# Mixer of a decoder trunk: pooling products regrouped, the neighbour's cut to 16 columns, and 30 unread products ahead of the first rows

## What is computed

```python
POOL_WINDOWS = (2, 4, 8, 16)          # one window for each group of 256 columns
def _pool_mixer(x, hist, w, scale):
    ...
    for g, win in enumerate(POOL_WINDOWS):
        xg = xs[..., g * POOL_GROUP:(g + 1) * POOL_GROUP].astype(jnp.float32)
        ...
        outs.append((c[:, j + 1] - c[:, lo]) / cnt[None, :, None] - xg[:, p_len:])
    d = jnp.stack(outs, axis=2).astype(x.dtype)
    y = jnp.einsum('blgc,gce->blge', d, w).reshape(x.shape)
    return y * scale
```

## Time and profile before

| | us |
|---|---|
| median of 3 runs | 2530.28 (2530.12 to 2531.79) |
| the profiled execution | 2531.07 |
| its span in the trace | 2529.3 |
| TensorE busy in the span | 2396.9 (95%) |
| VectorE, ScalarE, GpSimd busy | 1292.2, 768.9, 342.9 |

### The profile page before, as it was taken

How to read it: one execution, slowest core, us unless ns; L and a number is a source line. 1 busy time by engine, 2 the same in 40 slices (tenths; PEclk the granted TensorE clock), 3 DMA queues, 4 the chain that set the end, 5 groups by cost and what they waited for, 6 DMA issues and landing times.

```text
span 2529.3 us, 35338 instructions
## 1 busy us (share of the span) xinstructions
PE 2396.9 (95%) x14022; PEld 2183.7 (86%) x14022; DVE 1292.2 (51%) x2398; ACT 768.9 (30%) x1477; POOL 342.9 (14%) x345
## 2 busy tenths in 40 slices
PE   7899999999999888999989888899999999999997
PEld 7899999999999788889987667588998989899996
DVE  4733443333344685776768778635244343333336
ACT  2331111111111234555546555412311111111112
POOL 1400000000000341000006545033000000000006
PEclk9899999999999999999999999799999999999998
DMA  5121110111111031000005444411211111111111
GB/s 163 42 62 39 50 45 24 47 50 50 50 50 63 13 115 42 19 19 5 8 22 176 149 155 157 155 47 34 67 51 34 51 51 32 36 51 51 51 42 68
DMA packets 137083, 154.00 MB, mean 61 GB/s; under 512 B 10256, under 2 KB 114224, under 8 KB 136808
## 3 DMA queue, kind: packets, MB, share of 16 engines
q1 hardware_dynamic: 124656, 110.07, 13.9%
q0 software_dynamic: 12288, 41.95, 5.2%
HBM read 142.24 MB, written 10.32 MB: 60 GB/s over the span
## 4 chain that ended last, share of the span: by engine, by line
PE 84%; DVE 10%; ACT 3%; issue 2%; DMA 1%; POOL 0%; SPq 0%; ACTq 0%; DVEq 0%
PE ps L216 24%; PE ps L218 23%; PE ps L217 23%; DVE split L209 5%; PE ps L2161 2%; PE ps L2126 2%; ACT split L204 2%; PE ps L2141 1%; PE ps L224 1%; PE ps L223 1%; PE ps L2142 1%; PE ps L1671 1%; PE ps L2148 1%; PE ps L580 1%; DVE plain L1914 1%
## 5 line engine op out<-in xcount | busy, mean ns | idle before, releaser
L216 PE MATMUL ps<-split 128*128 128x512 f32 (+6 forms) x3632 | 1236.9, 341 | 45.3 <-DVE split L209 17.6
L217 PE MATMUL ps<-split 128*128 128x512 f32 (+6 forms) x3632 | 1223.4, 337 | 0.0
L218 PE MATMUL ps<-split 128*128 128x512 f32 (+6 forms) x3632 | 1223.0, 337 | 0.0
L216 PEld LDWEIGHTS ps<-split 128*128 128x128 f32 x3632 | 690.0, 190 | 89.7 <-DVE split L209 21.2
L217 PEld LDWEIGHTS ps<-split 128*128 128x128 f32 x3632 | 690.4, 190 | 39.1 <-issue 2.5
L218 PEld LDWEIGHTS ps<-split 128*128 128x128 f32 x3632 | 690.8, 190 | 37.3
L204 ACT ACTIVATE split<-plain 128x1024 fp32r<-128x1024 f32 (+9 forms) x454 | 314.6, 729 | 594.1 <-PE ps L224 365.6
L209 DVE TENSOR_TENSOR split<-plain,split 128x344 fp32r<-128x344 f32 (+7 forms) x430 | 372.4, 890 | 182.7 <-ACT split L204 179.7
L1000 DVE TENSOR_TENSOR plain<-plain,ps 128x350 f32<-128x350 f32 (+1 forms) x132 | 68.0, 515 | 557.7 <-ACT plain L954 557.1
L276 DVE TENSOR_TENSOR plain<-plain,ps 128x512 f32<-128x512 f32 x360 | 244.7, 685 | 194.2 <-PE ps L218 189.4
L209 DVE TENSOR_TENSOR split<-ps,split 128x512 fp32r<-128x512 f32 (+5 forms) x480 | 247.1, 554 | 137.2 <-ACT split L204 135.1
(11 more groups left out here) (147 smaller groups left out, 1450.3 us busy)
## 6 DMA issues: line engine op xcount, KB each, us to landing
plain<-w_gate SPq DMA_DIRECT2D x44, 512.0 KB, 4.7
plain<-w_up SPq DMA_DIRECT2D x44, 512.0 KB, 4.0
plain<-w_down SPq DMA_DIRECT2D x44, 512.0 KB, 4.3
plain<-x_prompt SPq DMA_DIRECT2D x8, 512.0 KB, 11.3
x_spill<-plain SPq DMA_DIRECT2D x1, 4096.0 KB, 14.5
plain<-wo SPq DMA_DIRECT2D x8, 512.0 KB, 4.7
plain<-x_spill SPq DMA_DIRECT2D x8, 512.0 KB, 8.5
y_prompt<-plain SPq DMA_DIRECT2D x8, 512.0 KB
```

The source lines that it names most:

```text
L216: pe.matmul(out, still[0], moving[0], start=start, stop=False)
L217: pe.matmul(out, still[0], moving[1], start=False, stop=False)
L218: return pe.matmul(out, still[1], moving[0], start=False, stop=stop)
```

## The change

Three things change, all in TensorE's part of the mixer, and one instruction is added on VectorE.

- `pool_half` no longer alternates own and neighbour: it issues the four own products of a half, then the four of the neighbour. Only the first product of a half has `start=True`, and only the last `stop=True`, so a bank holds one accumulation.
- The neighbour's product has 16 columns (`reach = WINDOWS[-1]`) where it had 128. Samples and meta rows keep 24.
- Ahead of its first wait for data, TensorE issues 30 products of 512 fp32r columns into bank 5, which nobody reads; VectorE fills their operand with 1.0 by one memset.

```diff
+def keep_busy(pe, k, times, bank, rows, width):
+    for _ in range(times):
+        pe.matmul(k.ps[:, bank, 0:width], rows[:, 0:P], rows[:, 0:width], start=True, stop=True)
 def mixer_pe(pe, k):
     s, nt = k.s, k.ns + k.nm
+    pe.wait_ge(s["warm"], 1)
+    keep_busy(pe, k, 30, UNIT_BANKS[1], k.xt_hi[:, 0, :], BANK)
     pe.wait_ge(s["kept_in"], 16)
...
-        for j in range(4):
-            kc = 4 * half + j
-            g, cols = kc // 2, slice(kc * P, (kc + 1) * P)
-            if t < k.tiles:
-                out = k.ps[:, POOLED_BANKS[half], j * P:(j + 1) * P]
-                pe.matmul(out, k.x_main[:, t, cols], k.pool_band("here", g), start=True, stop=False)
-                if t:
-                    mm = pe.matmul(out, k.x_main[:, t - 1, cols], k.pool_band("before", g), start=False, stop=True)
...
+        n = P if t < k.tiles else nt
+        reach = WINDOWS[-1] if t < k.tiles else nt
+        for own in (True, False):
+            for j in range(4):
+                kc = 4 * half + j
+                g, cols = kc // 2, slice(kc * P, (kc + 1) * P)
+                out = k.ps[:, POOLED_BANKS[half], j * n:(j + 1) * n]
+                if own and t < k.tiles:
+                    pe.matmul(out, k.x_main[:, t, cols], k.pool_band("here", g), start=j == 0, stop=False)
+                elif own:
+                    pe.matmul(out, k.hist[:, cols], k.pool_band("hist", g), start=j == 0, stop=False)
+                elif t == k.tiles:
+                    mm = pe.matmul(out, k.x_tail[0:nt, cols], k.pool_band("meta", g)[0:nt], start=False, stop=j == 3)
+                elif t:
+                    mm = pe.matmul(out[:, 0:reach], k.x_main[:, t - 1, cols], k.pool_band("before", g)[:, 0:reach],
+                                   start=False, stop=j == 3)
...
         @block.vector
         def _(dve):
+            dve.memset(k.xt_hi[:, 0, 0:BANK].bitcast(F32), 1.0).then_inc(k.s["warm"], 1)
             page_index_dve(dve, k)
```

More of the change, by code:

```diff
@@ L574, in pool_half @@
             pe.wait_ge(s["pooled_lo"], n - 1)
-        for j in range(4):
-            kc = 4 * half + j
-            g, cols = kc // 2, slice(kc * P, (kc + 1) * P)
-            if t < k.tiles:
-                out = k.ps[:, POOLED_BANKS[half], j * P:(j + 1) * P]
-                pe.matmul(out, k.x_main[:, t, cols], k.pool_band("here", g), start=True, stop=False)
-                if t:
-                    mm = pe.matmul(out, k.x_main[:, t - 1, cols], k.pool_band("before", g), start=False, stop=True)
-                else:
[L584 to L588, removed]
+        n = P if t < k.tiles else nt
[14 more added lines that the diff above has]
+                                   start=False, stop=j == 3)
+                else:
+                    mm = pe.matmul(out[:, 0:reach], k.x_tail[0:nt, cols], k.pool_band("meta_before", g)[0:nt, 0:reach],
+                                   start=False, stop=j == 3)
         mm.then_inc(s["pooled"], 1)
```

## The result

The changed kernel takes 2514.03 us, the median of 4 runs (2513.20 to 2518.18); the kernel before took 2530.62 beside it (4 runs, 2530.12 to 2531.79). The ratio is 0.9938, with a 95% interval of 0.9922 to 0.9953. So it is 16.6 us faster, and 8.6 were forecast. The profiled execution took 2513.20, its span 2511.4, where before had 2531.07 and 2529.3: 17.9 us in the two profiles that the rest of this text compares.

What follows compares the result with a forecast made beforehand. Tile 0's serial chain was taken to bound the mixer's start, then VectorE and ScalarE at 7.06 us a step, VectorE's queue its end. Sum 7.7 - 0.4 + 0.1 + 1.2 = 8.6 us: 2522, range 2518.5 to 2526.5.

Steps and rivals of the forecast that it cites:

- Part 1: Program start: the 30 unread products run beside the transfers, from about 1.3 us; cost 0 to 0.6 us, taken 0.
- Part 2: Mixer, tile 0: grouped products at full clock, neighbours 0.21 us each; fold at 15.9 instead of 23.67, gain 7.7 us.
- Part 3: Mixer from unit 0: the clock of the 30 products is gone again; cost 0.4 us, range -2 to +1.5.
- rival D: Mixer start: clock kept up to unit 0, units and half-tile 2 us faster, 2520 us; chance 7%.
- Part 4: Mixer, tiles 1 to 7: 0.1 us per step off TensorE, covered by VectorE's 7.06; gain taken 0.1 us.
- Part 5: Mixer, last tile's halves: 3.4 us instead of 6.9, so VectorE's wait of 1.24 goes; gain 1.2 us.
- Rival E: After tile 0: head start given back by an unseen wait, late data or VectorE's queue; 2526 to 2530 us; chance 6%.
- Rivals B: Program start: the 30 products, all slow, end at 14.1 and delay tile 0; 2526.5 to 2529 us; chance 6%.
- C: Tile 0 on time but slow, clock lost before 10.7 or rising later; 2523 to 2525.7 us; chance 9%.
- A: Mixer steps: narrow products cost the clock, some 5.3 us a step, 2554 us in the end; chance 4%.

Runs made afterwards that it cites:

- the wide kernel: The changed kernel with neighbour products of 128 columns instead of 16, still regrouped: 2514.33 us, ratio to before 0.9939.
- The run that kept the clock: The changed kernel with 23 more unread 512-column products, 5 behind tile 0's halves and 18 ahead of unit 0: 2513.84 us, ratio to before 0.9941.
- 8 and 12 tiny products: The kernel before with 8 or 12 unread products of 8 by 8 at the start, one run each: 2541.90 us with 8, 2544.62 us with 12.
- regrouping alone: The changed kernel without the 30 unread products, their wait and the memset; pooling products stay regrouped and narrowed: 2523.50 us, ratio to before 0.9982.
- the thirty tiny products: The kernel before with 30 unread products of 8 by 8 at the start: 2522.72 us, ratio 0.9978.
- the counter-test: The changed kernel with 98 further unread products of 8 by 8 behind the 30, 256 instructions together: 2524.21 us, ratio to before 0.9979.

## Why the prediction was wrong

**What bounds the kernel: right for the mixer.** The serial chain of tile 0 was the place to look; VectorE's step of 7.06 and its queue at the end set the rest.

**Part 1, the 30 products as work: right.** They start at 1.47 (forecast 1.3) and the first rows' products at 10.91 (before 10.70), so they cost 0.2 of the 0 to 0.6 allowed; in the second profile of the changed kernel these start at 11.26, which is all of the 0.6.

**Part 2, tile 0: right in its mechanism, 0.5 too good.** Half 0 was ready at 13.1, not 12.7: it began 0.1 later than assumed, four own products took 1.06 us and four neighbours 0.99, where 0.9 and 0.85 were taken. The neighbour with 24 rows costs 0.25, inside the 0.1 to 0.33; the one with 128 rows costs 0.82 / 4 = 0.205. The fold came 7.21 earlier, with 7.7 forecast. The Trainium skill ("TensorE: Matmul & The Clock Gate", Back-to-back issue gap) gives a product of up to 64 columns some 60 cycles. From that the prediction worked out near 0.1 us for a neighbour, an estimate; the rows at 30.24 and 31.06 show twice that, and the wide kernel the same for eight times the columns.

**Part 3, clock lost by unit 0: right.** The windows read 0.50 from 17.00 to 26.90. Unit 0 is 7.20 earlier and the second unit 7.08 (34.93 to 27.85), so the loss was 0.1 instead of 0.4. The run that kept the clock shows rival D's price: 2.55 us at the first addition, not kept.

**Part 4, narrowed and regrouped products of tiles 1 to 7: 0.1 forecast, nothing measured** (the 0.1 to 0.2 us that narrowing gives come from tile 0). **Part 5, the wait of 1.24 at the last tile: gone,** as forecast. The mixer ends 8.50 ahead of before; the sum said 8.6. The lead is 7.2 at 60 us, where the terms gave 7.4, and the end adds 1.3 where 1.2 were forecast. That the sum fits so well is partly luck: part 2 gave 0.5 less than forecast, and part 3 cost 0.3 less.

**The step that failed** is the last: "FFN products that began at 109.50 now near 101, and the same 8.6 at the end." The first half of it held, the second did not: the lead went from 8.3 at 1920 us to 18.0 at 2333. Part 1 counted the 30 products as time on TensorE and asked only what they stand in front of. They are also 60 instructions in the program, and this effect was none of the parts, of the rivals or of the range. Rival E asked whether a head start could be given back; that it could grow was left out. The trace of before had the rows: six waits for "issue" in FFN 1, 7.2 us together, and 102 packets on the instruction queue, of which 27 lie at three branches of a loop. To have said that they would vanish was not possible from the trace alone (8 and 12 tiny products make them longer), but it showed 7.2 us of stalls whose cause was not an engine or a transfer of the kernel's data. That belongs into the range on both sides for any edit that adds or takes instructions.

Rivals B and C did not happen, since tile 0 began at 10.91 and its first half took 2.05 us against 3.79 without the warm-up. Nor did A: a window of after over four of the steps with narrow products shows the granted clock at 1.00.

```profile
40.00:70.00 30.00, 30.00 (x262) 29.83 (x261) 23.86 (x59) 15.06 (x25) 19.76 (x9) 1.00 0.01 2
```

One caution on sizes. The runs of before spread from 2522.9 to 2538.3 (28 runs on one chip), so medians of single edits carry an error of 1 to 2 us; regrouping alone has 6.1 by its median and 9.8 in its profiled run. The split of the 17.9 us into 8.3 ahead of FFN 1 and 9.7 in it comes from two profiles. The second profile of the changed kernel has 8.2 at 135 us, 9.5 at the first landmark and the same 9.7 in FFN 1: the part in FFN 1 is firm, the lead ahead of it moves by a us or two from profile to profile. That the second part hangs on position rests on the thirty tiny products, whose interval against before excludes no effect, and on the counter-test, whose interval (0.9965 to 0.9993) lies wholly above that of the changed kernel (0.9922 to 0.9953).

## What to carry to other kernels

Read the waits for "issue" and the packets of the instruction queue, stage by stage, before costing an edit: where a long loop is fetched anew at each return, any edit that changes the number of instructions ahead of it, on that engine, may remove those stalls or bring them on. To know what an edit is worth by its own merit, measure it beside a version with equally many instructions that do nothing. Where a chain starts the program, put products with the same shape of weights next to each other and keep TensorE working ahead of them. By the end of the mixer the two gave 6.4 and 2.6 us alone and 9.0 together.

## What the runs showed of the hardware

- Whether a loop body of 1624 TensorE instructions was fetched anew at its returns depended on where it begins: at all three returns in before, 9 packets of 16,384 bytes and 2.6 to 3.9 us each time, at none in after, and at two places at some of them. 60 instructions of no work ahead of it were worth 7 us of 2530.
- Such a gap can be booked under another engine: with 12 tiny products it reads as 14.4 us of waiting for VectorE.
- A pooling product with new 128-row weights took 0.205 us with 16 columns and 0.20 with 128, at the full clock; with 24-row weights 0.25 and 0.27.
- Products that alternate between weight tiles of 128 and 24 rows cost 0.42 us each at the full clock and 0.72 at the lower one; grouped by shape they cost 0.25 to 0.28 and 0.45 to 0.50.
- The granted clock has no record before its first change: the column reads 1.00 over the slow first half-tile of regrouping alone as it did in before. The price of a known product tells the level there.
